# Late modulation blocks multiplied by VectorE during the first projection, ten places for row tiles in the first stage, and a mask of the band's edges

## The reference, cut to what matters

```python
def adaln_params(cond, w, b):
    m = jax.nn.silu(cond) @ w + b          # 1024 x 3072 weights per layer
    return jnp.split(m, 3, axis=-1)        # shift, scale, gate
...
hx = rms_norm(x, norm_g[layer]) * (1.0 + scx[:, None, :]) + shx[:, None, :]
hc = rms_norm(ctx, norm_g[layer]) * (1.0 + scc) + shc
ox, oc = even_mixer(hx, hc, ...)           # layer 0: projection, then window and differential attention
x = x + gtx[:, None, :] * (ox @ w_out[layer])
```

## Time and profile before

| what | value |
|---|---|
| median of 3 runs | 3582.53 us (3580.91 to 3591.55) |
| profiled execution, its own time | 3582.02 us |
| its span, first to last instruction | 3580.2 us |
| PE busy, of the span | 3224.9 us, 90% |
| DVE, ACT, POOL busy | 1679.7, 1237.7, 602.0 us |
| mean granted TensorE clock | 0.951 of full |
| `modulation` / `project_even` / `attention_even`, from the span's start | 0 to 95.4 / to 484 / to 970 us |

### The profile page before, as it was taken

One profiled execution on the slowest core, in us unless ns is written; L12 is line 12 of the kernel. 1 busy time (PEld: TensorE's weight loads), 2 busy tenths in 40 slices (PEclk: granted clock), 3 DMA queues, 4 the chain that ended last, 5 costly groups with the idle time before them and its releaser, 6 DMA issues. The chain is left out here.

```text
span 3580.2 us, 51447 instructions
## 1 busy us (share of the span) xinstructions
PE 3224.9 (90%) x20994; PEld 2819.0 (79%) x20994; DVE 1679.7 (47%) x2573; ACT 1237.7 (35%) x2267; POOL 602.0 (17%) x559
## 2 busy tenths in 40 slices
PE   5999968999798999897989997978779899999988
PEld 2999966777577999775878975667658799999877
DVE  3117716777565112165626215645555444554343
ACT  5223225555563334123524114543323211111232
POOL 1000019998011000111211110001200000000010
PEclk7999989999898999998999998989989899999999
DMA  5334361110154212233311335110012111111332
GB/s 174 105 105 157 127 233 43 53 60 36 61 194 133 78 59 78 91 106 138 118 47 43 92 100 126 37 7 2 2 67 77 53 47 47 46 42 53 117 129 94
DMA packets 192895, 302.21 MB, mean 84 GB/s; under 512 B 41848, under 2 KB 133752, under 8 KB 190652
## 3 DMA queue, kind: packets, MB, share of 16 engines
q1 hardware_dynamic: 169120, 213.13, 18.7%
q0 software_dynamic: 23584, 86.39, 7.3%
HBM read 226.33 MB, written 73.14 MB: 84 GB/s over the span
## 5 line engine op out<-in xcount | busy, mean ns | idle before, releaser
L115 PE MATMUL p_pb<-p_w_hi,h_hi 128*128 128x416 f32 (+2 forms) x1216 | 423.6, 348 | 6.5 <-DVE p_w_lo L110 6.5
L117 PE MATMUL p_pb<-p_w_hi,h_lo 128*128 128x416 f32 (+2 forms) x1216 | 421.9, 347 | 0.0
L116 PE MATMUL p_pb<-p_w_lo,h_hi 128*128 128x416 f32 (+2 forms) x1216 | 419.6, 345 | 0.0
L115 PE MATMUL fu_pf<-h_hi,fu_w_hi 128*128 128x344 f32 (+1 forms) x1056 | 339.5, 322 | 8.7 <-DVE fu_pf L3618 8.7
L116 PE MATMUL fu_pf<-h_lo,fu_w_hi 128*128 128x344 f32 (+1 forms) x1056 | 340.4, 322 | 0.0
L117 PE MATMUL fu_pf<-h_hi,fu_w_lo 128*128 128x344 f32 (+1 forms) x1056 | 338.9, 321 | 0.0
L115 PEld LDWEIGHTS p_pb<-p_w_hi,h_hi 128*128 128x128 f32 x1216 | 229.6, 189 | 7.7 <-issue 6.7
L116 PEld LDWEIGHTS p_pb<-p_w_lo,h_hi 128*128 128x128 f32 x1216 | 229.2, 188 | 2.4
L117 PEld LDWEIGHTS p_pb<-p_w_hi,h_lo 128*128 128x128 f32 x1216 | 228.9, 188 | 0.7
L115 PEld LDWEIGHTS fu_pf<-h_hi,fu_w_hi 128*128 128x128 f32 x1056 | 199.9, 189 | 9.1 <-DVE fu_pf L3618 9.1
L117 PEld LDWEIGHTS fu_pf<-h_hi,fu_w_lo 128*128 128x128 f32 x1056 | 199.8, 189 | 0.0
(11 more groups left out here) (545 smaller groups left out, 7212.2 us busy)
## 6 DMA issues: line engine op xcount, KB each, us to landing
fu_raw<-in_ffn_up SPq DMA_DIRECT2D x88, 256.0 KB, 3.1
fd_raw<-in_ffn_down SPq DMA_DIRECT2D x44, 512.0 KB, 3.5
att_mw<-in_adaln_w POOLq DMA_DIRECT2D x8, 2048.0 KB, 8.4
la_qkv<-p SPq DMA_DIRECT2D x16, 1024.0 KB, 5.0
p<-p_o SPq DMA_DIRECT2D x60, 208.0 KB, 1.9
s_raw<-in_w_in POOLq DMA_DIRECT2D x48, 256.0 KB, 3.6
rT<-p_stage SPq DMA_DIRECT2D x10, 896.0 KB, 5.0
p_raw<-in_ab_w_in POOLq DMA_DIRECT2D x10, 832.0 KB, 5.8
```

The source lines that it names most:

```text
L115: pe.matmul(out, left[0], right[0], start=start, stop=False)
L116: pe.matmul(out, left[0], right[1], start=False, stop=False)
L117: return pe.matmul(out, left[1], right[0], start=False, stop=stop)
```

## The change

- `modulation`: the ring of weight blocks has two places instead of three. All ten row tiles have a place of their own, and are normalized before the later loop; the multiplication by the reciprocal root goes from ACT to DVE (`spread`), which does it between its four `finish`. There are three places `y`.
- `project_even`: SP loads one 128 x 512 slab (256 KB) of the eight late blocks per step, in 64 of 72 steps, into two places; DVE multiplies and adds it, for one or two conditions, one step later: 14 multiplications and 98 fused multiply-adds. After eight slabs SP stores the sum to `sums` in HBM.
- `attention_even`: POOL loads a finished sum (512 KB or 256 KB) instead of a block, and only splits it. `pressed_at` moves: the eight sums over partitions come at the pairs 1, 4, 7 to 22 instead of 3, 7, 11 to 29.
- the window mask is held and loaded for the two outer blocks alone, and added by a matmul of 256 columns, written to PSUM with a gap, instead of 384.

```diff
+def mod_conds(i):
+    return 1 if MOD_LATER[i] in ((1, 4), (1, 5)) else 2
...
-    RING = 3
+    RING = 2
...
-    XR = 6
+    YR = 3
...
-        x = [ph.sb(f"x{s}", [P, D]) for s in range(XR)]
-        y = [ph.sb(f"y{s}", [P, KD, P]) for s in range(2)]
-        ss = [ph.sb(f"ss{s}", [P, 1]) for s in range(XR)]
+        x = [ph.sb(f"x{t}", [P, D]) for t in range(N)]
+        y = [ph.sb(f"y{s}", [P, KD, P]) for s in range(YR)]
+        ss = [ph.sb(f"ss{t}", [P, 1]) for t in range(N)]
...
                 def load_x(t):
-                    if t >= XR:
-                        pool.wait_ge(turned, t - XR + 1)
                     src = x_v[P * t:P * t + P, :] if t < NT else ctx_v[P * (t - NT):P * (t - NT) + P, :]
-                    pool.dma_start(x[t % XR][:, :], src).then_inc(x_in[t % XR], 16)
+                    pool.dma_start(x[t][:, :], src).then_inc(x_in[t], 16)
...
-                    s = t % XR
-                    act.wait_ge(x_in[s], 16 * (t // XR + 1))
-                    act.activation(hT[1][:, :, P * t:P * t + P], x[s][:, :].rearrange("p (k c) -> p k c", c=P), ACT.Square,
-                                   accum_out=ss[s][:, :]).then_inc(squared, 1)
+                    act.wait_ge(x_in[t], 16)
+                    act.activation(hT[1][:, :, P * t:P * t + P], x[t][:, :].rearrange("p (k c) -> p k c", c=P), ACT.Square,
+                                   accum_out=ss[t][:, :]).then_inc(squared, 1)
                     act.wait_ge(squared, t + 1)
-                    act.activation(ss[s][:, :], ss[s][:, :], ACT.Sqrt, scale=1.0 / D, bias=g.epsc[:, :]).then_inc(rooted, 1)
-                    act.wait_ge(recips, t + 1)
-                    act.activation(x[s][:, :], x[s][:, :], ACT.Copy, scale=ss[s][:, :]).then_inc(scaled, 1)
+                    act.activation(ss[t][:, :], ss[t][:, :], ACT.Sqrt, scale=1.0 / D, bias=g.epsc[:, :]).then_inc(rooted, 1)
...
-                    if t >= 2:
-                        act.wait_ge(lo_done, t - 1)
+                    if t >= YR:
+                        act.wait_ge(lo_done, t - YR + 1)
                     for k in on_act:
-                        ins = act.activation(y[s][:, k, :], pt[s][:, k, :], ACT.Identity, scale=cols[:, 1, k, c:c + 1], bias=cols[:, 0, k, c:c + 1])
+                        ins = act.activation(y[t % YR][:, k, :], pt[s][:, k, :], ACT.Identity, scale=cols[:, 1, k, c:c + 1], bias=cols[:, 0, k, c:c + 1])
...
-                for t in range(XR):
+                    act.activation(hT[0][:, :, P * t:P * t + P], y[t % YR][:, :, :], ACT.Copy).then_inc(hi_done, 1)
+                for t in range(N):
                     normalize(t)
                 for t in range(N):
                     affine(t)
-                    if t + XR < N:
-                        normalize(t + XR)
...
-                def recip(t):
+                def spread(t):
                     dve.wait_ge(rooted, t + 1)
-                    dve.reciprocal(ss[t % XR][:, :], ss[t % XR][:, :]).then_inc(recips, 1)
+                    dve.reciprocal(ss[t][:, :], ss[t][:, :]).then_inc(recips, 1)
+                    dve.wait_ge(recips, t + 1)
+                    dve.tensor_scalar(x[t][:, :], x[t][:, :], ss[t][:, :], None, ALU.mult).then_inc(scaled, 1)
...
-                for b in range(NB):
-                    if b < XR // 2:
-                        recip(2 * b)
-                        recip(2 * b + 1)
+                for b, t0 in enumerate((0, 2, 5, 8)):
+                    for t in range(t0, (0, 2, 5, 8, N)[b + 1]):
+                        spread(t)
                     finish(b)
...
-                    if t + XR < N:
-                        recip(t + XR)
...
+    def slab_at(step):
+        i, k = divmod(step, KD + 1)
+        return (i, k) if i < LATER and k < KD else None
+    def terms_before(i):
+        return sum(KD * mod_conds(q) for q in range(i))
...
+        slab = [ph.sb(f"slab{s}", [P, MOD_BLK]) for s in range(2)]
+        acc = ph.sb("acc", [P, 2, MOD_BLK])
...
+                def load_slab(i, k):
+                    if KD * i + k >= 2:
+                        before = KD * i + k - 1
+                        sp.wait_ge(termed, terms_before(before // KD) + mod_conds(before // KD) * (before % KD))
+                    layer, b = MOD_LATER[i]
+                    sp.dma_start(slab[k % 2][:, :], mod_w[:, k, layer, b, :]).then_inc(slab_in[k % 2], 16)
+                def store_sums(i):
+                    sp.wait_ge(termed, terms_before(i + 1))
+                    sp.dma_start(sums[i, :, 0:mod_conds(i), :], acc[:, 0:mod_conds(i), :]).then_inc(sums_out, 16)
...
+                    if slab_at(step):
+                        load_slab(*slab_at(step))
+                    if step and step % (KD + 1) == 0 and step // (KD + 1) <= LATER:
+                        store_sums(step // (KD + 1) - 1)
...
+                sp.wait_ge(sums_out, 16 * LATER)
...
+                def terms(i, k):
+                    n, at = mod_conds(i), terms_before(i) + mod_conds(i) * k
+                    dve.wait_ge(slab_in[k % 2], 16 * ((KD * i + k) // 2 + 1))
+                    if k == 0 and i:
+                        dve.wait_ge(sums_out, 16 * i)
+                    for c in range(n):
+                        one = g.act_c[:, k, c:c + 1]
+                        if k == 0:
+                            ins = dve.tensor_scalar(acc[:, c, :], slab[0][:, :], one, None, ALU.mult)
+                        else:
+                            dve.wait_ge(termed, at - n + c + 1)
+                            ins = dve.scalar_tensor_tensor(acc[:, c, :], slab[k % 2][:, :], one, acc[:, c, :], ALU.mult, ALU.add)
+                        ins.then_inc(termed, 1)
...
+                    if step and slab_at(step - 1):
+                        terms(*slab_at(step - 1))
...
-    w_v = a["adaln_w"].rearrange("l (k p) (b n) -> p k l b n", p=P, n=MOD_BLK)
...
-    pressed_at = {6 + 2 * n + 1: i for i, n in enumerate((3, 7, 11, 15, 19, 23, 26, 29))}
+    pressed_at = {6 + 2 * n + 1: i for i, n in enumerate((1, 4, 7, 10, 13, 16, 19, 22))}
...
-        mask_raw = ph.sb("mask_raw", [P, 3, W3])
-        mask = ph.ctx.enter_context(nc.sbuf_tensor("att_mask", [P, 3, W3], F32R))
...
-        mw = [ph.sb(f"mw{s}", [P, KD, MOD_BLK]) for s in range(2)]
-        acc = ph.sb("acc", [P, 2, MOD_BLK])
-        term = ph.sb("term", [P, 2, MOD_BLK])
+        acc = [ph.sb(f"acc{s}", [P, 2, MOD_BLK]) for s in range(2)]
...
-                    pool.dma_start(mask_raw[:, j, :], a["k_window"][t, :, :]).then_inc(small, 16)
+                    pool.dma_start(mask_raw[:, j, :, :], a["k_window"][t, :, :].rearrange("p (b k) -> p b k", b=3)[:, 0:3:2, :]).then_inc(small, 16)
...
                 def load(i):
-                    layer, b = MOD_LATER[i]
-                    pool.dma_start(mw[i % 2][:, :, :], w_v[:, :, layer, b, :]).then_inc(mw_in[i % 2], 16)
-                def accumulate(i):
-                    n, at, mws = conds(i), terms_before(i), mw[i % 2]
-                    pool.wait_ge(mw_in[i % 2], 16 * (i // 2) + 16)
-                    if i:
-                        pool.wait_ge(acc_split, i)
-                    for k in range(KD):
-                        for c in range(n):
-                            if k:
-                                pool.wait_ge(termed, at + n * (k - 1) + c + 1)
-                            pool.tensor_scalar((term if k else acc)[:, c, :], mws[:, k, :], g.act_c[:, k, c:c + 1], None,
-                                               ALU.mult).then_inc(scaled if k else termed, 1)
-                        for c in range(n if k else 0):
-                            pool.wait_ge(scaled, at - at // KD + n * (k - 1) + c + 1)
-                            pool.tensor_tensor(acc[:, c, :], acc[:, c, :], term[:, c, :], ALU.add).then_inc(termed, 1)
+                    pool.dma_start(acc[i % 2][:, 0:mod_conds(i), :], sums[i, :, 0:mod_conds(i), :]).then_inc(acc_in[i % 2], 16)
                 def split(i):
-                    n = conds(i)
+                    n, whole = mod_conds(i), acc[i % 2]
+                    pool.wait_ge(acc_in[i % 2], 16 * (i // 2) + 16)
                     if i:
                         pool.wait_ge(pressed, i)
-                    pool.tensor_copy(acc_hi[:, 0:n, :], acc[:, 0:n, :]).then_inc(acc_high, 1)
+                    pool.tensor_copy(acc_hi[:, 0:n, :], whole[:, 0:n, :]).then_inc(acc_high, 1)
                     pool.wait_ge(acc_high, i + 1)
-                    lo_part(pool, acc_lo[:, 0:n, :], acc[:, 0:n, :], acc_hi[:, 0:n, :]).then_inc(acc_split, 1)
+                    lo_part(pool, acc_lo[:, 0:n, :], whole[:, 0:n, :], acc_hi[:, 0:n, :]).then_inc(acc_split, 1)
...
-                    accumulate(i)
-                    pool.wait_ge(termed, terms_before(i + 1))
+                    split(i)
                     if i + 2 < LATER:
+                        pool.wait_ge(acc_split, i + 1)
                         load(i + 2)
-                    split(i)
...
```

(5 more changed lines are left out.)

40 lines of the change are left out of this document (21 added, 19 removed).

## The result

The kernel after takes 3547.6 us (median of 4 runs, 3546.6 to 3555.0), beside 3587.0 for the kernel before on the same chip (median of 4): a ratio of 0.989, 95% interval 0.9857 to 0.9923. Run once more beside other kernels it gave 0.9893 (0.9877 to 0.9909). The forecast was 3553, with a range of 3542 to 3569. The profiled executions are 3582.0 before and 3547.4 after, 34.6 us apart.

A forecast was written before the change was run, and what follows sets the result against it. PE was taken as the bound, so gains come only where it waits. From 3582.0 us, minus 6.1 (first stage), 0.0 (projection) and 19.5 + 0.7 + 3.3 (attention) gave 3552.4, stated as 3553, range 3542 to 3569.

The forecast's parts named there:

- What bounds the kernel: Whole kernel: PE is busy 3224.9 of 3580.2 us, so work taken from another engine pays only where PE waits.
- Attention, contention: Attention: POOL's SBUF work delays DVE and PE; taking most of it away shortens 31 periods from 396.3 to 376.8, 19.5 us less.
- The pattern of the sums: Attention: of the eight sums over partitions, seven cost 1.24 us over the floor and one 3.26, 11.9 us together.
- The 0.7 us for the first pair and the context units: Start of the attention: these are disturbed by POOL too, and were given a gain of 0.7 us.
- The mask: Attention's window units: two matmuls lose 128 columns each, 51 ns a matmul, 3.3 us less in all.
- First projection: Projection: DVE has room for the added terms, any lateness is covered for some 14 us, so no time is counted.
- First stage: First stage: later weights start the tile loop 11.7 us late, the shorter loop saves 17.8; net 6.1 us less.
- The slow start: First stage: after idling, PE runs seven passes of block 3 at the slow pace, making the tile loop 11.7 us late, not 8.7.
- Splits collide after every sum: Rival, attention: POOL's split collides with DVE's multiply-add at every sum, costing 14 us: 3567; chance 0.14.
- The first stage gives nothing: Rival, first stage: block 4 lands late or the tile loop stays at 3.8 us a tile: 3559 to 3565; chance 0.14.
- The slab ring paces the projection: Rival, projection: slow slab landings, from 9 us on, hold up SP's stores, ACT and PE; some 48 us lost, 3600; chance 0.05.
- Nothing arrives: Rival, whole kernel: POOL's loss was mostly behind PE's own work and the first stage gives nothing: 3572; chance 0.05.

The follow-up runs named there:

- the mixed run: Kernel after, sums at their old places, GpSimd repeating 112 multiplications and 112 additions on private buffers without the 2 MB loads: 3577.1 us, ratio 0.9973.
- The doubled terms: Kernel after with each of the 98 fused multiply-adds of the projection's sums done twice: 3565.9 us, ratio 0.9937.

## Why the prediction was right

**What bounds the kernel: right.** Time came back where TensorE had waited, in the first stage and in the attention, and for 3.7 us where its own work shrank, at the mask. VectorE's 71 us more in the projection cost nothing.

**Attention, contention: right in mechanism, and in size within 2 us.** The sum said 376.8 us for 31 periods, less 3.2 for the mask: 373.6. Measured 371.4. The run with the whole mask gives the first number by itself: 376.5. The pattern of the sums was read a little wrong. I took one at 3.26; it was 1.66, and the 3.26 of the earlier trace rows held a stretch at half clock. Nor did the split there begin before the multiply-add, as I wrote: in the trace of before the cast starts at 892.31, 0.03 us behind it, and it is the subtraction at 893.00 that falls into it. I counted the 1.24 of the others as what a sum and the split behind it cost together; the eighth sum, without a split beside it, shows that the sum alone costs this, through VectorE's bias addition behind its multiply-add.

The 0.7 us for the first pair and the context units did not come: from the start of the attention to the first maximum it was 1.4 us more. TensorE's granted clock is 0.50 from 521 to 533 us in that stretch; whether this is the cause no run shows. That "both engines read SBUF" is now sharper: it takes two tensor operands on VectorE and a reading instruction on GpSimd.

Of the loss before I cannot give the exact share of each cause: the mixed run, whose instructions fall in other places, lost about 11 us by contention, the kernel before 31.4 less 8 sums of 1.23, some 21.5. The holds differ in the same measure: over their bare time VectorE's three lines of 128x2 instructions took 31.2 us in all before and 17.2 in the mixed run (548 to 920 us). So nothing here asks for a share of the 2 MB loads, which the mixed run leaves out, but no run shows them alone.

**The mask: right.** 51 ns a matmul expected, 57 measured; 3.3 us expected, 31 x 0.12 = 3.7 measured.

**First projection: right, with a thinner cover than the words suggest.** Landing 3.2 us (3.1 expected), terms 0.745 (0.75), densest stretch 50.6 of 53 us (54 expected). TensorE's time changed by 0.1 us. The doubled terms show where the lateness appears, and their 10.6 us of waiting agree with a cover of some 14 us.

**First stage: right in its parts, 3 to 5 us off in size.** Block 3 began at 38.66 (38.2 expected), TensorE ended at 54.15 (55.0, since four passes were slow and not seven), the tile loop started at 57.53 (58.4). The step that failed is the loop's period: "1.37 for its half, 1.23 for the low part and two gaps, 2.8 us a tile". It is 2.41. There are no gaps: on VectorE each instruction starts 0.08 us before the one ahead ends, as the rows above show (1.36 + 1.21 - 0.16). 9 x 0.39 = 3.5 us, the shorter tail 0.9 and the start 0.9 are the difference of 5.2: the last low part ends 11.3 us earlier, not 6.1. The period is 2.41 in every trace with this stage. The start is not as firm: the loop begins at 57.5 to 60.0 us in the ten traces, and 58.4 lies among them, so that the 0.9 of the start is chance. The slow start was the right choice against a fast one. The rule of the Trainium skill (TensorE: Matmul & The Clock Gate, What's actually happening) that an idle TensorE falls to 1.2 GHz agrees with the trace of after: behind 9.43 us of idle time the granted clock of 38 to 42 us is 0.51.

```profile
38.00:42.00 4.00, 3.34 (x5) 0.49 (x6) 0.00 (x0) 0.81 (x3) 0.00 (x0) 0.51 1.04 393
```

**The rivals.** *Splits collide after every sum*: they do meet, but with two-condition blocks the one that is held up is GpSimd's cast, off TensorE's path. Only the short cast of a one-condition block lets the subtraction get in the way, for 0.4 us. *The first stage gives nothing*: no. *The slab ring paces the projection*: no, and even with one place it does not; a landing near the 7.5 us that I gave as the limit for two places was not tried. *Nothing arrives*: no.

The total: 29.6 us expected against 34.6 between the profiled executions. The difference of 5.0 is mostly that of the first stage (10.8 against 6.1); in the attention the smaller length of the periods (24.9 against 22.8) and the longer way to the first maximum nearly cancel, which is luck.

## What to carry to other kernels

Before you move work from GpSimd to VectorE, look at VectorE's shortest instructions with two tensor operands in the stage that GpSimd accompanies: if some take 0.5 to 2 us instead of 0.16, and TensorE waits behind them, the GpSimd work costs its contention and not its length. Put work where an engine has room and nobody near waits for it, then double it once on the chip to learn how thick the cover is. A small addition can set the time of a sum by where it stands: here the bias addition waits behind a multiply-add of 1.55 us, and halving TensorE's products changed nothing. For a loop bound by one engine, take the period from start to start of its own instructions, not from durations plus gaps.

## What was not expected of the hardware

- VectorE's instruction with two tensor operands in SBUF that starts during an addition of two tensors on GpSimd ends when that addition ends (0.94 us instead of 0.16 at 713.04 us). During a multiplication by a number it is held only until 0.70 of its 1.56 us. Memsets (0.95 us of 128x1024, 193 of them in the stretch) never held it, and VectorE's instructions with one tensor operand were never held. The other way round GpSimd's cast waited for VectorE's multiply-add, 1.95 us instead of 1.04.
- A short wait can cost more than itself, and does not always: behind a wait of 1.24 us at the seventh sum TensorE's granted clock was 1.00 in the kernel after and 0.61 with the whole mask, whose period of 15.02 us lost 1.6 us by it. The kernel with the first stage alone had periods of 16 to 18.6 us.
- A matmul that adds into a PSUM row with a block of 128 columns left out keeps the whole gain of having fewer columns: 333 ns for 256 columns with the gap, 390 for 384 without.
